# Scores of the latent attention from stacked operands: two products of 128 rows and three of 32 rows for each unit

## The chip, the core and the metric

One core of a Trainium2 chip runs the whole kernel in one launch. The metric is the device time of one execution in microseconds (us). The engines are named as in the profile: PE is TensorE's matmul, PEld its weight load, DVE VectorE, ACT ScalarE, POOL GpSimd, and SP SyncE, whose only work here is to issue DMAs.

## The reference, cut to what matters

The program is a two-layer trunk. Its second layer has a latent attention with 16 heads, 1024 query tokens and 1280 keys (256 of context and 1024 of the sequence). The score of a head has two parts: 64 dimensions of its own ("nope") and 32 rotated dimensions ("rope"), whose keys are shared by all heads.

```
C_HEADS = 16
C_NOPE = 64
C_ROPE = 32
...
def mla_block(q_nope, q_pe, k_nope, k_pe, v):
    scale = (C_NOPE + C_ROPE) ** -0.5
    s = (jnp.einsum('bhqd,bhkd->bhqk', q_nope, k_nope)
         + jnp.einsum('bhqr,bkr->bhqk', q_pe, k_pe)).astype(jnp.float32) * scale
    p = jax.nn.softmax(s, axis=-1)
    return jnp.einsum('bhqk,bhkd->bhqd', p.astype(v.dtype), v)
```

All of it is float32. The kernel splits q and k into a rounded part `hi` and a rest `lo`, and takes hi·hi + hi·lo + lo·hi for a product.

## The kernel before

`project_heads` computes q, k and v and stores them in DRAM, q and k as hi and lo parts: 64 rows for each head's nope dimensions, and behind them the rope rows (32 for each head in q, 32 in all in k). `latent_attention` then goes through 128 units. A unit is one head and 128 query tokens, so a head has 8 units; its scores are 128 x 1280, in three chunks of keys (512, 512 and 256 wide), one PSUM bank each. Two units make a pair, and there are 64 pairs.

A chunk of scores is one `exact_product`: three matmuls (lines 88, 89 and 90) over 96 rows (64 nope and 32 rope rows, stacked). DVE takes the maximum of a unit's scores (line 2956), ACT the exponential (line 2926). PE turns the 10 blocks of 128 x 128 of the result in three groups of 4, 4 and 2 (`turned`, line 2870, with one more block in line 2874 for the inverse sums), ACT and DVE copy them out of PSUM (lines 2934 and 2964), and PE multiplies a pair's blocks with the values (`product`, line 2888). That product goes, for the two units of the pair, to two column halves of 64 each. DVE multiplies it with the inverse sums (`output`, line 2980).

Each engine has its own program, and semaphores join them. PE's order in a pair p is written out by hand; a = 2p and b = 2p + 1 are its units, and scores run two units ahead. A unit's scores need the exponential of the unit two before, since there are two score buffers. Turned groups and products take turns in two PSUM banks: `bank_free` makes PE wait until the fill two before has been read. So group 0 of unit b waits for `output(p - 1)` on DVE, since the product is the fill two before it, and group 1 of unit b waits for ACT's copy of group 2 of unit a.

SP loads a head's q and k with `load_head`: 6 DMAs on one side of a double buffer, issued when the last unit of the head before the one in use has its scores, which is 8 units ahead of their use. The first head's operands are loaded already in `project_heads` (with the shared rope rows, 8 DMAs, `FIRST_LOADS`).

Of the kernel before, what the change touches and what calls it, by code (L numbers as in the profile page):

```python
# [9 lines left out]
F32 = mybir.dt.float32  # L10
# [5 lines left out]
P = 128  # L16
# [20 lines left out]
C_NOPE = 64  # L37
C_ROPE = 32
C_V = 64
C_Q_RANK = 768  # L40
C_KV_RANK = 256
C_IN = C_Q_RANK + C_KV_RANK + C_ROPE
# [41 lines left out]
def exact_product(pe, out, a_hi, a_lo, b_hi, b_lo, first, last):  # L84

    pe.matmul(out, a_hi, b_hi, start=first, stop=False)  # L88
    pe.matmul(out, a_hi, b_lo, start=False, stop=False)  # L89
    return pe.matmul(out, a_lo, b_hi, start=False, stop=last)  # L90
# [2270 lines left out]
                        pool.tensor_tensor(rstd, ms, minus_half[:, :], ALU.pow).then_inc(s.p_rstd.sem, 1)  # L2361


FIRST_LOADS = 8


def load_head(sp, h, q, k, q_parts, k_parts, signal):

    for dst, src in ((k[0], k_parts[0]), (q[0], q_parts[0]), (q[1], q_parts[1]), (k[1], k_parts[1])):
        sp.dma_start(dst[0:C_NOPE, :].bitcast(F32), src[h * C_NOPE:(h + 1) * C_NOPE, :]).then_inc(signal, 16)  # L2370
    first = C_HEADS * C_NOPE + h * C_ROPE
    for dst, src in zip(q, q_parts):
        sp.dma_start(dst[C_NOPE:C_NOPE + C_ROPE, :].bitcast(F32), src[first:first + C_ROPE, :]).then_inc(signal, 16)


def load_positions(sp, k, k_parts, signal):

    for dst, src in zip(k, k_parts):
        sp.dma_start(dst[C_NOPE:C_NOPE + C_ROPE, :].bitcast(F32),
                     src[C_HEADS * C_NOPE:C_HEADS * C_NOPE + C_ROPE, :]).then_inc(signal, 16)  # L2380


def project_heads(nc, q_parts, k_parts, v_rows, cq, ckv, k_pe, w_uq, w_ukv, cos, sin, turn, q_first, k_first, first_in):


    CK, KK = C_Q_RANK // P, C_KV_RANK // P
    HD = C_NOPE + C_ROPE
    SCALE = HD ** -0.5
    k_chunks, q_chunks = token_chunks(T), token_chunks(SEQ)
    GROUP = 4  # L2390
# [348 lines left out]

def latent_attention(nc, y_hi, y_lo, q_parts, k_parts, v_rows, ident, w_raw, w_out, q_first, k_first, first_in):  # L2740

    HD = C_NOPE + C_ROPE
    KT = TT
    UNITS = C_HEADS * XT
    PAIRS = UNITS // 2
# [28 lines left out]
    with ExitStack() as ctx:  # L2774
        def sb(label, shape, dt=F32):
            return ctx.enter_context(nc.sbuf_tensor(f"mla_{label}", shape, dt))

        qs = q_first, [sb(f"q_{n}", [HD, SEQ], F32R) for n in ("hi", "lo")]
        ks = k_first, [sb(f"k_{n}", [HD, T], F32R) for n in ("hi", "lo")]
        v = sb("v", [P, 2, KT, C_V])  # L2780
        e = sb("e", [P, E_SLOTS, T])
        pt = sb("pt", [P, 2, 2, KT, P])
# [6 lines left out]
        s_ps = ctx.enter_context(nc.psum_tensor("mla_scores", [P, 2, 3 * BANK], F32))  # L2789
        t_ps = ctx.enter_context(nc.psum_tensor("mla_turned", [P, 2, BANK], F32))  # L2790
        s = ctx.enter_context(stage(nc, "mla", [
            "pe_in", "qk0_in", "qk1_in", "v0_in", "v1_in", "w_in", "s_full", "max", "exp", "inverted", "inv_spread", "t_full",
            "copied_vector", "copied_scalar", "o_done", "y_rounded", "y_done"], inherited=[first_in]))
        qk_in, v_in = (s.qk0_in, s.qk1_in), (s.v0_in, s.v1_in)
        QK_LOADS = 6
        block = ctx.enter_context(nc.Block())

        @block.sync
        def _(sp):
            def head(h):  # L2800
                if h >= 2:
                    sp.wait_ge(s.s_full.sem, (h - 1) * XT)
                load_head(sp, h, qs[h % 2], ks[h % 2], q_parts, k_parts, qk_in[h % 2].sem)

            def values(h):
                if h >= 2:
                    sp.wait_ge(s.o_done.sem, (h - 1) * PER_HEAD)
                sp.dma_start(v[:, h % 2, :, :],
                             v_rows.rearrange("(t p) n -> p t n", p=P)[:, :, h * C_V:(h + 1) * C_V])\
                  .then_inc(v_in[h % 2].sem, 16)  # L2810

            values(0)
            load_positions(sp, ks[1], k_parts, s.pe_in.sem)
            head(1)
            values(1)
            for h in range(2, C_HEADS):
                head(h)
                values(h)
                if h == 4:
                    for k in range(KD):  # L2820
                        sp.dma_start(w_raw[:, k, :], w_out[k * P:(k + 1) * P, :]).then_inc(s.w_in.sem, 16)
            sp.wait_ge(s.w_in.sem, 16 * KD)

        @block.tensor
        def _(pe):
            def scores(n, c):
                h, t = divmod(n, XT)
                if n >= UNITS:
                    return
                if c == 0:  # L2830
                    if n == 0:
                        pe.wait_ge(first_in, 16 * FIRST_LOADS)
                    elif t == 0:
                        pe.wait_ge(qk_in[h % 2].sem, 16 * QK_LOADS * ((h + 1) // 2))
                        if h == 1:
                            pe.wait_ge(s.pe_in.sem, 32)
                    if n >= 2:
                        pe.wait_ge(s.exp.sem, n - 1)
                a, width = chunks[c]
                tokens = slice(t * P, (t + 1) * P)  # L2840
                (q_hi, q_lo), (k_hi, k_lo) = qs[h % 2], ks[h % 2]
                mm = exact_product(pe, s_ps[:, n % 2, a:a + width], q_hi[:, tokens], q_lo[:, tokens],
                                   k_hi[:, a:a + width], k_lo[:, a:a + width], True, True)
                if c == len(chunks) - 1:
                    mm.then_inc(s.s_full.sem, 1)

            def bank_free(f):

                pair, at = divmod(f - 2, FILLS)
                if f < 2:  # L2850
                    return
                if at == PRODUCT and pair == 0:
                    at = 0
                if at == PRODUCT:
                    pe.wait_ge(s.o_done.sem, pair)
                    return
                unit, group = ((0, 0), (0, 1), None, (0, 2), (1, 0), (1, 1), (1, 2))[at]
                vector, scalar = copies(pair * 2 + unit, group)
                if (unit, group) in by_vector:
                    pe.wait_ge(s.copied_vector.sem, vector)  # L2860
                else:
                    pe.wait_ge(s.copied_scalar.sem, scalar)

            def turned(n, g):
                f = fill(n, g)
                if g == 0:
                    pe.wait_ge(s.exp.sem, n + 1)
                bank_free(f)
                for m, kt in enumerate(groups[g]):
                    mm = pe.transpose(t_ps[:, f % 2, m * P:(m + 1) * P], e[:, n % E_SLOTS, kt * P:(kt + 1) * P],  # L2870
                                      ident[:, :])
                if n % 2 and g == 2:
                    pe.wait_ge(s.inv_spread.sem, n // 2 + 1)
                    mm = pe.transpose(t_ps[:, f % 2, 2 * P:3 * P], inv_rows[:, n // 2 % 2, :], ident[:, :])
                mm.then_inc(s.t_full.sem, 1)

            def product(pair):
                f = product_fill(pair)
                h = pair // PER_HEAD
                bank_free(f)  # L2880
                vector, scalar = copies(2 * pair + 1, 2)
                pe.wait_ge(s.copied_vector.sem, vector)
                pe.wait_ge(s.copied_scalar.sem, scalar)
                if pair % PER_HEAD == 0:
                    pe.wait_ge(v_in[h % 2].sem, 16 * (h // 2 + 1))
                for kt in range(KT):
                    for half in range(2):
                        mm = pe.matmul(t_ps[half * C_V:(half + 1) * C_V, f % 2, 0:P], v[:, h % 2, kt, :],
                                       pt[:, pair % 2, half, kt, :], start=kt == 0, stop=kt == KT - 1)
                mm.then_inc(s.t_full.sem, 1)  # L2890

            for n in range(2):
                for c in range(len(chunks)):
                    scores(n, c)
            for p in range(PAIRS):
                a, b = 2 * p, 2 * p + 1
                scores(a + 2, 0)
                turned(a, 0)
                scores(a + 2, 1)
                turned(a, 1)  # L2900
                scores(a + 2, 2)
                if p:
                    product(p - 1)
                turned(a, 2)
                scores(b + 2, 0)
                turned(b, 0)
                scores(b + 2, 1)
                turned(b, 1)
                scores(b + 2, 2)
                turned(b, 2)  # L2910
            product(PAIRS - 1)
# [119 lines left out]
def trunk(nc, i, consts, ropes, out):  # L3031
# [15 lines left out]
    with ExitStack() as ctx:  # L3047
# [42 lines left out]
        mla_v = scratch("mla_v", T, C_HEADS * C_V)  # L3090
        with ExitStack() as layer1:
            first_head = ExitStack()
            q_first, k_first = ([first_head.enter_context(nc.sbuf_tensor(f"{name}_first_{part}", [C_NOPE + C_ROPE, n],
                                                                     F32R, side="right")) for part in ("hi", "lo")]
                                for name, n in (("q", SEQ), ("k", T)))
            first_in = nc.alloc_semaphore(name="first_in")
            project_heads(nc, q_parts, k_parts, mla_v, cq, ckv, k_pe, i.c_w_uq[0], i.c_w_ukv[0], ropes[2], ropes[3],
                          turn_c, q_first, k_first, first_in)
# [53 lines left out]
```

## Time and profile before

| what | value |
|---|---|
| time of three runs | median 3620.37 us (3615.41 to 3621.24) |
| the profiled execution | 3610.87 us, its span 3609.1 us |
| mean granted TensorE clock | 0.960 of full speed |
| latent attention in the span | from 2200.6 us to about 2741 us, 540 us |
| PE busy over the whole span | 3310.6 us, 92% |

The span goes from the first to the last instruction of one execution. Busy time of PE is taken from modelled ends of pipelined matmuls, so a matmul's duration is longer than its share of a steady stream: the stream is read from the starts of neighbouring instructions.

### The profile page before, as it was taken

Reading aid. Unit: us, or ns where it says so; the run is one execution under the profiler, and the core shown is the slowest. Engines: PE = TensorE matmul, PEld = TensorE weight load, DVE = VectorE, ACT = ScalarE, POOL = GpSimd, SP = SyncE. Lnnn points to the kernel's source line nnn. Section 1 sums busy time; section 2 is a strip of 40 time slices with the busy share of each in tenths; the row PEclk is TensorE's granted clock in tenths of the full one; section 3 lists DMA queues with packets and bytes.
Section 4 is the critical chain, followed back from the end, with each engine's and each line's share of the span. In section 5 each row is a group of like instructions: output and inputs, shape, how many; then the busy total and the mean of one; then the engine's idle time right before and its main releaser. Section 6 shows DMA issues by size and latency. Waiting matters only on the chain. (4 is left out here: it accounts for less than half of the span.)

```text
span 3609.1 us, 47628 instructions
## 1 busy us (share of the span) xinstructions
PE 3310.6 (92%) x18952; PEld 2774.3 (77%) x18952; DVE 1823.9 (51%) x2092; ACT 1166.5 (32%) x1908; POOL 294.7 (8%) x527
## 2 busy tenths in 40 slices
PE   3999599798999999999979698999999799999998
PEld 1787477677888888888869577888887688888886
DVE  4599666454344443444453434555554444444446
ACT  2212155456211111111146323555554322112122
POOL 1000000112000000000012111111111200000001
PEclk6999799889999999999989899999999899999999
DMA  4322587242211111111042743322212311111113
GB/s 183 80 84 98 161 280 245 100 126 87 55 53 35 35 35 35 35 41 41 30 136 84 278 156 94 103 56 49 60 41 77 77 59 52 47 46 58 35 47 117
DMA packets 277081, 316.29 MB, mean 88 GB/s; under 512 B 83824, under 2 KB 222672, under 8 KB 275904
## 3 DMA queue, kind: packets, MB, share of 16 engines
q1 hardware_dynamic: 264160, 267.09, 24.8%
q0 software_dynamic: 12768, 47.08, 3.5%
q8 instruction: 106, 1.74, 0.2%
q14 instruction: 47, 0.39, 0.0%
HBM read 243.54 MB, written 70.58 MB: 87 GB/s over the span
## 5 line engine op out<-in xcount | busy, mean ns | idle before, releaser
L1102 DVE TENSOR_TENSOR y_sum<-ffn_down_ps,y_sum 128x512 f32<-128x512 f32 x396 | 271.1, 690 | 235.7 <-PE ffn_down_ps L90 235.0
L88 PE MATMUL ffn_gate_ps<-y_hi,ffn_w_hi 128*128 128x512 f32 (+1 forms) x880 | 325.5, 370 | 19.0 <-DVE ffn_w_lo L1055 19.0
L88 PE MATMUL ffn_down_ps<-ffn_w_hi,ffn_act_hi 128*128 128x512 f32 x792 | 312.4, 394 | 16.8 <-DVE y_sum L1102 10.4
L89 PE MATMUL ffn_gate_ps<-y_lo,ffn_w_hi 128*128 128x512 f32 (+1 forms) x880 | 325.1, 369 | 0.0
L90 PE MATMUL ffn_gate_ps<-y_hi,ffn_w_lo 128*128 128x512 f32 (+1 forms) x880 | 324.7, 369 | 0.0
L89 PE MATMUL ffn_val_ps<-y_lo,ffn_w_hi 128*128 128x512 f32 (+1 forms) x880 | 323.9, 368 | 0.0
L88 PE MATMUL ffn_val_ps<-y_hi,ffn_w_hi 128*128 128x512 f32 (+1 forms) x880 | 323.8, 368 | 0.0
L90 PE MATMUL ffn_val_ps<-y_hi,ffn_w_lo 128*128 128x512 f32 (+1 forms) x880 | 323.7, 368 | 0.0
L89 PE MATMUL ffn_down_ps<-ffn_w_lo,ffn_act_hi 128*128 128x512 f32 x792 | 309.4, 391 | 0.0
L90 PE MATMUL ffn_down_ps<-ffn_w_hi,ffn_act_lo 128*128 128x512 f32 x792 | 309.1, 390 | 0.0
L1055 DVE TENSOR_TENSOR ffn_w_lo<-ffn_raw,ffn_w_hi 128x1024 fp32r<-128x1024 f32 x132 | 158.0, 1223 | 286.4 <-ACT ffn_w_hi L1014 286.4
L1035 ACT ACTIVATE ffn_act_hi<-ffn_conv 128x1024 fp32r<-128x1024 f32 x66 | 53.4, 840 | 593.3 <-DVE ffn_conv L1082 593.3
L2956 DVE TENSOR_REDUCE mla_neg_max<-mla_scores 128x1 f32<-128x1280 f32 x128 | 190.2, 1486 | 52.6 <-PE mla_scores L90 52.6
L1068 DVE TENSOR_SCALAR ffn_conv<-ffn_gate,ffn_taps 128x1281 f32<-128x1281 f32 (+1 forms) x44 | 38.8, 883 | 341.7 <-ACT ffn_gate L1024 341.7
L2870 PE MATMUL mla_turned<-ident,mla_e 128*128 128x128 f32 x1280 | 206.3, 275 | 1.9 <-ACT mla_pt L2934 1.3
L2926 ACT ACTIVATE mla_e<-mla_scores,mla_neg_max 128x1280 f32<-128x1280 f32 x128 | 170.0, 1328 | 111.6 <-DVE mla_neg_max L2956 111.6
L88 PEld LDWEIGHTS ffn_gate_ps<-y_hi,ffn_w_hi 128*128 128x128 f32 x880 | 166.7, 189 | 48.0 <-DVE ffn_w_lo L1055 19.8
L1014 ACT ACTIVATE ffn_w_hi<-ffn_raw 128x1024 fp32r<-128x1024 f32 x132 | 134.4, 1048 | 209.2 <-PE ffn_val_ps L90 195.6
L88 PEld LDWEIGHTS ffn_down_ps<-ffn_w_hi,ffn_act_hi 128*128 128x128 f32 x792 | 149.1, 188 | 59.1 <-DVE y_sum L1102 21.9
L2870 PEld LDWEIGHTS mla_turned<-ident,mla_e 128*128 128x128 f32 x1280 | 156.2, 141 | 48.1 <-issue 11.8
L666 DVE SCALAR_TENSOR_TENSOR ab_conv<-ab_u,ab_taps,ab_conv 128x1295 f32<-128x1295 f32 x120 | 188.1, 1567 | 3.2
L89 PEld LDWEIGHTS ffn_gate_ps<-y_lo,ffn_w_hi 128*128 128x128 f32 x880 | 166.7, 189 | 28.1
(299 smaller groups left out, 7007.0 us busy)
## 6 DMA issues: line engine op xcount, KB each, us to landing
ffn_raw<-in_ffn_w_up SPq DMA_DIRECT2D x88, 512.0 KB, 3.8
da_ada_w<-in_ada_w SPq DMA_DIRECT2D x10, 4096.0 KB, 24.8
ffn_raw<-in_ffn_w_down SPq DMA_DIRECT2D x44, 512.0 KB, 5.7
ab_raw<-in_ab_w_in SPq DMA_DIRECT2D x20, 512.0 KB, 3.8
mod_ada_w<-in_ada_w SPq DMA_DIRECT2D x4, 2048.0 KB, 11.3
scratch_mla_q_hi<-up_out_hi POOLq DMA_DIRECT2D x12, 512.0 KB, 2.9
scratch_mla_q_lo<-up_out_lo POOLq DMA_DIRECT2D x12, 512.0 KB, 3.2
scratch_qk_hi<-ab_qk_hi POOLq DMA_DIRECT2D x8, 640.0 KB, 3.2
```

Source lines behind the costliest of these rows:

```text
L88: pe.matmul(out, a_hi, b_hi, start=first, stop=False)
L89: pe.matmul(out, a_hi, b_lo, start=False, stop=False)
L90: return pe.matmul(out, a_lo, b_hi, start=False, stop=last)
L666: dve.scalar_tensor_tensor(out=out, in0=src[:, j:j + SPAN], scalar=taps[:, i, j:j + 1], in1=out, op0=ALU.mult, op1=ALU.add)\
L1014: act.activation(w_hi[:, kind, :], raw[:, kind, :], ACT.Copy).then_inc(s.w_hi_done, 1)
L1035: act.activation(act_hi[:, slot, b:b + m], conv[:, padded(b):padded(b) + m], ACT.Copy)\
L1055: dve.tensor_tensor(w_lo[:, kind, :], raw[:, kind, :], w_hi[:, kind, :].bitcast(F32), ALU.subtract).then_inc(s.w_ready, 1)
L1068: dve.tensor_scalar(inner, gate[:, 1:PAD - 1], here, bias, ALU.mult, ALU.add)\
L1102: dve.tensor_tensor(part, down_ps[:, half, :], part, ALU.add).then_inc(s.sum_done, 1)
L2870: mm = pe.transpose(t_ps[:, f % 2, m * P:(m + 1) * P], e[:, n % E_SLOTS, kt * P:(kt + 1) * P], ident[:, :])
L2926: act.activation(e[:, n % E_SLOTS, :], s_ps[:, n % 2, 0:T], ACT.Exp, bias=neg_max[:, n:n + 1], accum_out=sums[:, n:n + 1]).then_inc(s.exp. ...
L2956: dve.tensor_reduce(neg_max[:, n:n + 1], s_ps[:, n % 2, 0:T], AX.X, ALU.max, negate=True)\
```

## The change

The rows of hi·hi, hi·lo and lo·hi (3 x 96 for each chunk) are stacked anew, as 128, 128 and 32. The left operand of product 0 is q's nope hi (64 rows), q's rope hi (32) and the first 32 rows of q's nope lo; of product 1 it is q's nope hi, q's rope hi and the second 32 rows of q's nope lo. The right operands are k's nope hi, k's rope hi and the first 32 rows of k's nope hi; and k's nope lo, k's rope lo and the second 32 rows of k's nope hi. What is left is q's rope lo with k's rope hi, 32 rows. For each chunk that is one matmul more, and the three chunks take it from three separate groups of 32 rows (0 to 31, 32 to 63, 64 to 95), for which q's rope lo is loaded three times and k's rope hi is laid out once as `k_rope`.

```
-                mm = exact_product(pe, s_ps[:, n % 2, a:a + width], q_hi[:, tokens], q_lo[:, tokens],
-                                   k_hi[:, a:a + width], k_lo[:, a:a + width], True, True)
+                q, k = qs[h % 2], ks[h % 2]
+                for m in range(2):
+                    pe.matmul(s_ps[:, n % 2, a:a + width], q[m][:, tokens], k[m][:, a:a + width], start=m == 0,
+                              stop=False)
                 if c == len(chunks) - 1:
+
+                    for m, (a, width) in enumerate(chunks):
+                        rows = slice(m * BLOCK, (m + 1) * BLOCK)
+                        mm = pe.matmul(s_ps[:, n % 2, a:a + width], q[2][rows, tokens], k_rope[rows, 0:width],
+                                       start=False, stop=True)
                     mm.then_inc(s.s_full.sem, 1)
```

A head's loads become 13 DMAs (for the first head 15 with the shared rows), and three loads of `k_rope` stand first in SP's program of the stage; unit 0's scores wait for them:

```
+HEAD_LOADS = 13
+POSITION_LOADS = 2
+FIRST_LOADS = HEAD_LOADS + POSITION_LOADS
...
+    for n in range(2):
+        some = slice(h * C_NOPE + n * BLOCK, h * C_NOPE + (n + 1) * BLOCK)
+        load(k[n], 0, k_parts[n], nope)
+        load(q[n], 0, q_parts[0], nope)
+        load(q[n], C_NOPE, q_parts[0], rope)
+        load(q[n], HD, q_parts[1], some)
+        load(k[n], HD, k_parts[0], some)
+    for n in range(3):
+        load(q[2], n * BLOCK, q_parts[1], rope)
...
+            for c, (a, width) in enumerate(chunks):
+                sp.dma_start(k_rope[c * BLOCK:(c + 1) * BLOCK, 0:width].bitcast(F32),
+                             k_parts[0][C_HEADS * C_NOPE:C_HEADS * C_NOPE + C_ROPE, a:a + width])\
+                  .then_inc(s.rope_in.sem, 16)
...
                     if n == 0:
                         pe.wait_ge(first_in, 16 * FIRST_LOADS)
+                        pe.wait_ge(s.rope_in.sem, 16 * len(chunks))
```

And the order of PE's work in a pair is another. Six blocks of scores become three:

```
             for p in range(PAIRS):
                 a, b = 2 * p, 2 * p + 1
-                scores(a + 2, 0)
                 turned(a, 0)
-                scores(a + 2, 1)
+                for c in range(len(chunks)):
+                    scores(a + 2, c)
                 turned(a, 1)
-                scores(a + 2, 2)
                 if p:
                     product(p - 1)
                 turned(a, 2)
                 scores(b + 2, 0)
                 turned(b, 0)
+                turned(b, 1)
                 scores(b + 2, 1)
-                turned(b, 1)
                 scores(b + 2, 2)
                 turned(b, 2)
```

On PE, from the last chunk of unit a's scores to group 0 of unit b, the program before reads:

```order
L88 MATMUL mla_scores<-k_first_hi,q_first_hi 128x256
L89 MATMUL mla_scores<-k_first_lo,q_first_hi 128x256
L90 MATMUL mla_scores<-k_first_hi,q_first_lo 128x256
L2888 MATMUL mla_turned<-mla_pt,mla_v 64x128 x20
L2870 MATMUL mla_turned<-ident,mla_e 128x128 x2
L88 MATMUL mla_scores<-k_first_hi,q_first_hi 128x512
L89 MATMUL mla_scores<-k_first_lo,q_first_hi 128x512
L90 MATMUL mla_scores<-k_first_hi,q_first_lo 128x512
L2870 MATMUL mla_turned<-ident,mla_e 128x128 x4
```

And the changed one, from unit a's scores to the end of unit b's (line 2861 is now the product over 128 rows, line 2867 the one over 32 rows, 2894 `turned`, 2912 `product`):

```order
L2861 MATMUL mla_scores<-k_first,q_first 128x512 x4
L2861 MATMUL mla_scores<-k_first,q_first 128x256 x2
L2867 MATMUL mla_scores<-mla_k_rope,q_first 128x512 x2
L2867 MATMUL mla_scores<-mla_k_rope,q_first 128x256
L2894 MATMUL mla_turned<-ident,mla_e 128x128 x4
L2912 MATMUL mla_turned<-mla_pt,mla_v 64x128 x20
L2894 MATMUL mla_turned<-ident,mla_e 128x128 x2
L2861 MATMUL mla_scores<-k_first,q_first 128x512 x2
L2894 MATMUL mla_turned<-ident,mla_e 128x128 x8
L2861 MATMUL mla_scores<-k_first,q_first 128x512 x2
L2861 MATMUL mla_scores<-k_first,q_first 128x256 x2
L2867 MATMUL mla_scores<-mla_k_rope,q_first 128x512 x2
```

Between the product of the values and group 0 of unit b stood three matmuls of 512 columns, and now stand two; each unit has a block of 32-row products between its scores and the next turned group.

On SP, at the start of the stage, the program before reads (the values of head 0, the shared rows, then head 1):

```order
L2808 DMA mla_v<-scratch_mla_v 128x10x64
L2379 DMA mla_k_hi<-scratch_mla_k_hi 32x1280
L2379 DMA mla_k_lo<-scratch_mla_k_lo 32x1280
L2370 DMA mla_k_hi<-scratch_mla_k_hi 64x1280
L2370 DMA mla_q_hi<-scratch_mla_q_hi 64x1024
```

and the changed one:

```order
L2826 DMA mla_k_rope<-scratch_mla_k_hi 32x512 x2
L2826 DMA mla_k_rope<-scratch_mla_k_hi 32x256
L2821 DMA mla_v<-scratch_mla_v 128x10x64
L2394 DMA mla_k_first<-scratch_mla_k_hi 32x1280
L2394 DMA mla_k_second<-scratch_mla_k_lo 32x1280
L2378 DMA mla_k_first<-scratch_mla_k_hi 64x1280
L2378 DMA mla_q_first<-scratch_mla_q_hi 64x1024
```

The three loads of `k_rope` moved in ahead of everything else.

## Rows read from the trace of the kernel before

**Rows 1.** Windows: busy us of each engine (count), PE clock, DMA share, GB/s
```profile
2200.00:2741.00 541.00, 534.57 (x5056) 466.99 (x5056) 314.91 (x448) 305.35 (x577) 90.06 (x192) 1.00 0.26 59
2300.00:2400.00 100.00, 100.00 (x953) 87.56 (x954) 59.06 (x85) 57.37 (x109) 17.01 (x36) 1.00 0.37 98
```

**Rows 2.** Timeline (start us, us, engine ...): one pair, from product to next product
```profile
2349.86 0.28 PE L90 MATMUL mla_scores<-k_first_hi,q_first_lo 96*128 96x256 f32 x1
...
2350.07 2.40 PE L2888 MATMUL mla_turned<-mla_pt,mla_v 128*64 128x128 f32 x40
...
2352.40 0.44 PE L2870 MATMUL mla_turned<-ident,mla_e 128*128 128x128 f32 x2
...
2352.92 0.40 PE L89 MATMUL mla_scores<-k_first_lo,q_first_hi 96*128 96x512 f32 x1
...
2353.39 0.60 PE L2870 MATMUL mla_turned<-ident,mla_e 128*128 128x128 f32 x4
...
2355.08 0.28 PE L89 MATMUL mla_scores<-k_first_lo,q_first_hi 96*128 96x256 f32 x1
...
2355.20 0.28 PE L90 MATMUL mla_scores<-k_first_hi,q_first_lo 96*128 96x256 f32 x1
...
2355.32 0.38 PE L2870 MATMUL mla_turned<-ident,mla_e 128*128 128x128 f32 x2
...
2358.35 2.40 PE L2888 MATMUL mla_turned<-mla_pt,mla_v 128*64 128x128 f32 x40
```

**Rows 3.** One tile: durations min/median/max ns of the product with the values
```profile
L2888 PE MATMUL mla_turned<-mla_pt,mla_v x2560: 272/273/324, 2217.3 to 2739.4; 128*64 128x128 f32 x197
```

**Rows 4.** Timeline in the projection: matmuls on 128 rows, then on 32
```profile
2011.60 0.28 PE L89 MATMUL up_main<-up_ckv_lo,up_wkv_hi 128*128 128x256 f32 x1
2011.72 0.28 PE L90 MATMUL up_main<-up_ckv_hi,up_wkv_lo 128*128 128x256 f32 x1
2011.93 1.90 PE L2543 MATMUL up_main<-up_k_pe,turn_c 32*32 32x512 f32 x4
```

**Rows 5.** One line: durations min/median/max ns of those on 32 rows
```profile
L2543 PE MATMUL up_main<-up_k_pe,turn_c x4: 588/588/612, 2011.9 to 2013.2; 32*32 32x512 f32 x4
```

**Rows 6.** Timeline: scores after a wait, so that the weight load is bare
```profile
2207.18 0.50 PE L88 MATMUL mla_scores<-k_first_hi,q_first_hi 96*128 96x512 f32 x1 [1.11 <-ACT mla_e L2926]
...
2207.52 0.40 PE L89 MATMUL mla_scores<-k_first_lo,q_first_hi 96*128 96x512 f32 x1
```

**Rows 7.** Timeline in the last pair: product, output, group 0 of unit b
```profile
2731.52 2.40 PE L2888 MATMUL mla_turned<-mla_pt,mla_v 128*64 128x128 f32 x40 [0.79 <-DVE mla_pt L2964]
...
2733.97 0.59 DVE L2980 TENSOR_TENSOR mla_o<-mla_turned,mla_inv_t 64x128 f32<-64x128 f32 x2 [1.46 <-PE mla_turned L2888]
...
2734.71 1.06 PE L2870 MATMUL mla_turned<-ident,mla_e 128*128 128x128 f32 x8 [0.42 <-DVE mla_o L2980]
```

**Rows 8.** The page, costliest groups: busy us, mean ns of one | idle before
```profile
L2956 DVE TENSOR_REDUCE mla_neg_max<-mla_scores 128x1 f32<-128x1280 f32 x128 | 190.2, 1486 | 52.6 <-PE mla_scores L90 52.6
...
L2926 ACT ACTIVATE mla_e<-mla_scores,mla_neg_max 128x1280 f32<-128x1280 f32 x128 | 170.0, 1328 | 111.6 <-DVE mla_neg_max L2956 111.6
```

**Rows 9.** Timeline at the stage's start, and loads: KB each, us to landing
```profile
2200.57 0.38 SPq L2808 DMA_DIRECT2D mla_v<-scratch_mla_v  x1
2200.61 0.76 PE L88 MATMUL mla_scores<-k_first_hi,q_first_hi 96*128 96x512 f32 x1 [11.06 <-PEq L76]
...
ident<-in_squares SPq DMA_DIRECT2D x1, 64.0 KB, 1.9
...
mla_k_hi<-scratch_mla_k_hi SPq DMA_DIRECT2D x1, 160.0 KB, 4.1
```

**Rows 10.** Timeline of SP: a head's six loads (first, last), the next heads' first
```profile
2231.01 0.45 SPq L2370 DMA_DIRECT2D k_first_hi<-scratch_mla_k_hi  x1
...
2234.33 0.42 SPq L2373 DMA_DIRECT2D q_first_lo<-scratch_mla_q_lo  x1
...
2264.24 0.45 SPq L2370 DMA_DIRECT2D mla_k_hi<-scratch_mla_k_hi  x1
```

More of the change, by code:

```diff
@@ L39 @@
 C_V = 64
+HD = C_NOPE + C_ROPE
 C_Q_RANK = 768
@@ L2361, in _, with load @@
                         pool.tensor_tensor(rstd, ms, minus_half[:, :], ALU.pow).then_inc(s.p_rstd.sem, 1)
-FIRST_LOADS = 8
+HEAD_LOADS = 13
+POSITION_LOADS = 2
+FIRST_LOADS = HEAD_LOADS + POSITION_LOADS
 def load_head(sp, h, q, k, q_parts, k_parts, signal):
[L2369 to L2373, printed above, removed]
+    nope = slice(h * C_NOPE, (h + 1) * C_NOPE)
+    rope = slice(C_HEADS * C_NOPE + h * C_ROPE, C_HEADS * C_NOPE + (h + 1) * C_ROPE)
+    def load(dst, at, src, rows):
+        sp.dma_start(dst[at:at + rows.stop - rows.start, :].bitcast(F32), src[rows, :]).then_inc(signal, 16)
+    for n in range(2):
[7 more added lines that the diff above has]
+        load(q[2], n * BLOCK, q_parts[1], rope)
 def load_positions(sp, k, k_parts, signal):
     for dst, src in zip(k, k_parts):
-        sp.dma_start(dst[C_NOPE:C_NOPE + C_ROPE, :].bitcast(F32),
+        sp.dma_start(dst[C_NOPE:HD, :].bitcast(F32),
                      src[C_HEADS * C_NOPE:C_HEADS * C_NOPE + C_ROPE, :]).then_inc(signal, 16)
@@ L2386, in project_heads @@
     CK, KK = C_Q_RANK // P, C_KV_RANK // P
-    HD = C_NOPE + C_ROPE
     SCALE = HD ** -0.5
@@ L2740, in latent_attention @@
 def latent_attention(nc, y_hi, y_lo, q_parts, k_parts, v_rows, ident, w_raw, w_out, q_first, k_first, first_in):
-    HD = C_NOPE + C_ROPE
     KT = TT
@@ L2776, in sb @@
             return ctx.enter_context(nc.sbuf_tensor(f"mla_{label}", shape, dt))
-        qs = q_first, [sb(f"q_{n}", [HD, SEQ], F32R) for n in ("hi", "lo")]
-        ks = k_first, [sb(f"k_{n}", [HD, T], F32R) for n in ("hi", "lo")]
+        qs = q_first, [sb(f"q_{n}", [P, SEQ], F32R) for n in ("first", "second", "rope")]
+        ks = k_first, [sb(f"k_{n}", [P, T], F32R) for n in ("first", "second")]
+        k_rope = sb("k_rope", [HD, BANK], F32R)
         v = sb("v", [P, 2, KT, C_V])
@@ L2791, in latent_attention @@
         s = ctx.enter_context(stage(nc, "mla", [
-            "pe_in", "qk0_in", "qk1_in", "v0_in", "v1_in", "w_in", "s_full", "max", "exp", "inverted", "inv_spread", "t_full",
+            "pe_in", "rope_in", "qk0_in", "qk1_in", "v0_in", "v1_in", "w_in", "s_full", "max", "exp", "inverted", "inv_spread", "t_full",
             "copied_vector", "copied_scalar", "o_done", "y_rounded", "y_done"], inherited=[first_in]))
         qk_in, v_in = (s.qk0_in, s.qk1_in), (s.v0_in, s.v1_in)
-        QK_LOADS = 6
         block = ctx.enter_context(nc.Block())
@@ L2832, in scores @@
                         pe.wait_ge(first_in, 16 * FIRST_LOADS)
+                        pe.wait_ge(s.rope_in.sem, 16 * len(chunks))
                     elif t == 0:
-                        pe.wait_ge(qk_in[h % 2].sem, 16 * QK_LOADS * ((h + 1) // 2))
+                        pe.wait_ge(qk_in[h % 2].sem, 16 * HEAD_LOADS * ((h + 1) // 2))
                         if h == 1:
-                            pe.wait_ge(s.pe_in.sem, 32)
+                            pe.wait_ge(s.pe_in.sem, 16 * POSITION_LOADS)
                     if n >= 2:
@@ L2840, in scores @@
                 tokens = slice(t * P, (t + 1) * P)
-                (q_hi, q_lo), (k_hi, k_lo) = qs[h % 2], ks[h % 2]
-                mm = exact_product(pe, s_ps[:, n % 2, a:a + width], q_hi[:, tokens], q_lo[:, tokens],
-                                   k_hi[:, a:a + width], k_lo[:, a:a + width], True, True)
+                q, k = qs[h % 2], ks[h % 2]
+                for m in range(2):
+                    pe.matmul(s_ps[:, n % 2, a:a + width], q[m][:, tokens], k[m][:, a:a + width], start=m == 0,
+                              stop=False)
                 if c == len(chunks) - 1:
+                    for m, (a, width) in enumerate(chunks):
+                        rows = slice(m * BLOCK, (m + 1) * BLOCK)
+                        mm = pe.matmul(s_ps[:, n % 2, a:a + width], q[2][rows, tokens], k_rope[rows, 0:width],
+                                       start=False, stop=True)
                     mm.then_inc(s.s_full.sem, 1)
@@ L2896, in _ @@
                 a, b = 2 * p, 2 * p + 1
-                scores(a + 2, 0)
                 turned(a, 0)
-                scores(a + 2, 1)
+                for c in range(len(chunks)):
+                    scores(a + 2, c)
                 turned(a, 1)
-                scores(a + 2, 2)
                 if p:
@@ L2906, in _ @@
                 turned(b, 0)
+                turned(b, 1)
                 scores(b + 2, 1)
-                turned(b, 1)
                 scores(b + 2, 2)
@@ L3092, in trunk @@
             first_head = ExitStack()
-            q_first, k_first = ([first_head.enter_context(nc.sbuf_tensor(f"{name}_first_{part}", [C_NOPE + C_ROPE, n],
-                                                                     F32R, side="right")) for part in ("hi", "lo")]
-                                for name, n in (("q", SEQ), ("k", T)))
+            q_first, k_first = ([first_head.enter_context(nc.sbuf_tensor(f"{name}_first_{part}", [P, n], F32R,
+                                                                     side="right")) for part in range(parts)]
+                                for name, n, parts in (("q", SEQ, 3), ("k", T, 2)))
             first_in = nc.alloc_semaphore(name="first_in")
```

## The prediction

> **What bounds the kernel now.** First the windows [rows 1]: from 2200 to 2741 us PE is busy for 534.57 of 541 us, in the middle of the stage for all of it, at a granted clock of 1.00 (2.4 GHz). DVE and ACT are busy for 315 and 305 us, a good half. So the stage is PE's stream of instructions, and a gain or a loss on PE goes straight into the time, unless it opens a wait. Then the timeline of one pair, read by starts [rows 2]. From one product to the next it is 2358.35 - 2350.07 = 8.28 us. In it a score matmul of 512 columns takes (2353.39 - 2352.92) / 2 = 0.235 us and one of 256 columns (2355.32 - 2355.08) / 2 = 0.12. Four turned blocks start 0.11 apart ((0.60 - 0.27) / 3), and product to next turned group is 2.33. With 12 x 0.235 + 6 x 0.12 = 3.54 of scores, 19 turned blocks at 0.11 (2.09), the product (2.33), the two blocks behind it (0.27) and 0.09 ahead of it (below) the pair is accounted for to 0.04 us: there are no waits to win.
>
> **Two things in that stream price the change.** One is that parts of the array work side by side: 40 instructions of the product start within 2.40 - 0.27 = 2.13 us, one in 0.055 us, although each streams 128 columns of float32, for which a turned block takes 0.11. They are two column halves. The other is what it costs to go there and back. From the last score matmul to the first of the product it is 2350.07 - 2349.86 = 0.21 instead of 0.12, so 0.09 more; the first matmul there lasts 324 instead of 273 ns [rows 3], 0.05 more. On the way back the last product matmul starts at 2350.07 + 2.13 = 2352.20 and the turned block at 2352.40, 0.20 instead of 0.11, and the two turned blocks last 0.44 instead of 0.38: 0.09 + 0.06 [rows 2].
>
> Is that so for 32 rows too? The trace has one place, a matmul of 32 rows and 32 columns behind matmuls of 128 rows: 2011.93 - 2011.72 = 0.21 against 0.12 [rows 4], the same 0.09, and its first lasts 24 ns longer than the others (612 against 588, [rows 5]). That is 24 ns for 32 columns of weights and 51 for 64; with 128 columns it should be 0.10, and a score matmul that finds its weights unloaded does last 0.50 instead of 0.40 [rows 6]. So I take 0.09 on entry, 0.10 for the weights and 0.15 on the way out: 0.34 us each time. The row changes rows and columns at once; that rows alone pay the same I infer.
>
> The Trainium skill says, in "TensorEngine Tiling (Array Packing)", Key Properties, that changing the tiling mode, and not just the tile, drains TensorE. The trace agrees where it has such a change, with 0.09 us at the entry. By the rule each unit pays 0.34 us; without it the block of 32 rows would cost its stream alone, as in rival B.
>
> **The change on PE.** For each of the 128 units it removes one of three matmuls for each chunk: 2 x 0.235 + 0.12 = 0.59 us. It adds three matmuls of 32 rows. If they run side by side they take one stream of 512 columns, 0.235, and 0.01 for the later starts. With 0.34 for the change there and back that is 0.585. Net 0.005 a unit, 0.6 us in all: nothing. The products over 128 rows instead of 96 I take at the same time. The fewer changes between scores and turned blocks gain nothing either, since those show no gap in the account above.
>
> Bounds: without any cost of the change the block is 0.245 (gain 0.345 a unit, 44 us); side by side but with three weight loads in turn it is 0.10 longer (third load 0.20 late but only 0.12 of stream, second 0.10 late and 0.235), 13 us in all; with the products in turn it is 0.235 + 0.12 longer, 45 us.
>
> **The new order.** Group 0 of unit b needs `output` of the pair before. In the last pair, where PE has nothing else to do, it starts 2734.71 - 2731.52 = 3.19 us after the product did, released by that DVE work [rows 7]. Before the change it started at 2353.39, 3.32 after the product: 0.13 to spare. Now two, not three, matmuls of 512 columns stand in between, so PE is there at 3.32 - 0.235 = 3.085 and waits 0.105. In 62 pairs that is 6.5 us, whatever the 32 rows cost. Nothing gives it back, since PE is the bound and the turned groups behind it queue up. The other waits keep their cover: ACT's copy of unit a's group 2, for which group 1 of unit b waits, stands behind an exponential. From the end of unit a + 2's scores it is 1.49 of maximum and 1.33 of exponential [rows 8], and the copy, with the gaps between engines some 3.8 us; PE has 0.44 + 2.33 + 0.27 + 0.47 + 0.44 and the wait in between, 4.05. DVE's copy of group 0, queued behind a maximum, needs 1.49 and the copy from the end of unit b's scores; PE has 0.33 + 0.44 + 1.77 + 0.44 = 3.0 until the product wants that bank.
>
> **SP and the loads.** At the start PE began at 2200.61, when SP only issued its first load [rows 9]. Now unit 0 waits for `k_rope`: third issue 2 x 0.43 later, and a load of 64 KB lands 1.9 us after its issue, 2.8 in all. A load of 160 KB in the stage took 4.1, which would make 5. I take 3.0. Nothing else is on the chip then to hide it. The values of head 0 stand behind them, but their product comes at 2217.3 [rows 3]. A head's loads grow from 6 to 13: the six take 2234.75 - 2231.01 = 3.7 us to issue [rows 10], so 13 take 8, and a load lands some 4 later [rows 9]. The next head's scores start 33.2 us after the issue (2264.24 - 2231.01), so some 20 us are to spare. Bytes grow by about 1.7 for these loads, against a DMA share of 0.26 [rows 1]. The first head's loads, 15 for 8, are issued in the projection as soon as its rows are stored, while PE goes through the other heads' products. All that is hidden, at 0.
>
> **Sum.** 0 + 6.5 + 3.0 = 9.5 us. The profiled execution of 3610.87 us becomes 3620.4, and the median of the runs, 3620.37, which lies 9.5 above that execution, becomes 3629.9. A measurement of this kernel tells some 0.2%, 7 us, from no change, so this would be just slower.
>
> **The rivals.**
>
> B, the rows change nothing: PE takes the block of 32 rows without the cost seen at the column halves, since only rows differ. For it speaks that scores over 96 rows and turned blocks over 128 alternate without any gap [rows 2]; against it the 0.21 of [rows 4]. 9.5 - 44 = -35 us, 3586. The side changes where the block costs less than 0.515 a unit. By the Trainium skill ("TensorE: Matmul & The Clock Gate", Part 3, The mechanism) a weight load for other row groups is pulled ahead of matmuls in flight, which is this case; no row of this trace shows it for rows alone.
>
> B', half of it: one of the two changes is covered or the weights of 32 rows load during the entry. The block costs 0.10 to 0.17 less, 13 to 22 us: 3608 to 3617, faster or the same.
>
> C, the weights of the three load in turn: the block is 0.10 longer, 9.5 + 13 = +22, 3643. Against it speaks that the column halves' first two matmuls cost 0.05 together, the load of one.
>
> D, the three products don't overlap, as the change says they would: 0.355 longer a unit, +45 + 9.5, 3675. What the product shows is overlap of columns; rows into three separate banks are untried in this trace.
>
> Same, the wait at group 0 is not there, because the output's release comes 0.1 sooner than in the last pair, or the entry is a little cheaper: 3623.
>
> **How the numbers follow.** The likeliest, full cost and side by side, has 0.42, and its own range is 3625 to 3638 (block of 0.56 to 0.62, `k_rope` up to 5 us, the wait up to 0.13). B has 0.20, B' 0.14, the last case 0.08, C 0.10, D 0.06. Faster by over 0.2% are B and half of B': 0.27. Slower are C, D and 0.38 of the likeliest: 0.54. The rest, 0.19, is within 0.2%. Leaving out D and the ends of the others, the range is 3585 to 3644.
>
> **What the profile after would show.** Right: two matmuls over 128 rows 0.235 apart, then 0.21 to the first of 32 rows, the three of them starting together and the first lasting 0.10 longer than an ordinary one; the turned block 0.32 or so after their start plus load; PE waiting 0.1 us for `mla_o` before group 0 of unit b; PE's first matmul some 3 us after SP's first load; a pair of 8.4 us. Wrong: a block of 0.25 (pair of 7.7, B), starts of the three 0.235 apart (D) or 0.10 apart (C), or a wait for qk loads at a head's first unit.

## The result and the profile after

| | before | changed |
|---|---|---|
| median of 7 runs | 3620.37 us (3615.41 to 3622.56) | 3630.56 us (3627.06 to 3634.32) |
| ratio | | 1.0031, 95% interval 1.0021 to 1.0040 |
| profiled execution, its span | 3610.87, 3609.1 | 3632.77, 3631.0 |
| a pair: mean distance of neighbouring products' starts, pairs 3 to 58 | 8.302 us | 8.417 us |
| first to last product of the stage | 520.03 us | 526.76 us |
| SP's first load of the stage to PE's first matmul | 0.04 us | 2.79 us |

The change costs 10.2 us, 0.3%. The latent attention accounts for it: 526.76 - 520.03 = 6.7 us between its products and 2.75 at its start are 9.5 us. The two profiled executions lie 21.9 us apart, but 12.4 of these are outside the stage: 8.7 before it and 3.7 behind it. It began at 2209.29 instead of 2200.57, and before that the two programs do the same work but for the first head's seven more loads. In the other kernels with this projection the stage began between 2202.1 and 2213.5. In all of them the difference arose in the projection's first 80 us or earlier, before those loads are issued. So the loads are not its cause, and the medians, 10.2 us apart, leave at most a small part of it to the change. From the last product to the end of the span all ten kernels do the same work, and take between 871 and 876 us. Whether there is such a part the two profiled executions with the old projection (before and e5_order_alone, with stage starts at 2200.57 and 2205.68, and both at the lower end behind the stage) don't settle.

The timeline of the changed kernel, one pair from the end of unit a's scores on (start us, us, engine, line; compare [rows 2]):

```profile
2732.36 0.28 PE L2861 MATMUL mla_scores<-mla_k_first,mla_q_first 128*128 128x256 f32 x1
2732.48 0.28 PE L2861 MATMUL mla_scores<-mla_k_second,mla_q_second 128*128 128x256 f32 x1
2732.69 0.50 PE L2867 MATMUL mla_scores<-mla_k_rope,mla_q_rope 32*128 32x512 f32 x3
2733.12 0.66 PE L2894 MATMUL mla_turned<-ident,mla_e 128*128 128x128 f32 x4
...
2733.70 2.40 PE L2912 MATMUL mla_turned<-mla_pt,mla_v 128*64 128x128 f32 x40
...
2736.04 0.44 PE L2894 MATMUL mla_turned<-ident,mla_e 128*128 128x128 f32 x2
2736.15 0.59 DVE L3003 TENSOR_TENSOR mla_o<-mla_turned,mla_inv_t 64x128 f32<-64x128 f32 x2 [1.23 <-PE mla_turned L2912]
...
2736.55 0.40 PE L2861 MATMUL mla_scores<-mla_k_second,mla_q_second 128*128 128x512 f32 x1
...
2736.89 0.52 PE L2894 MATMUL mla_turned<-ident,mla_e 128*128 128x128 f32 x3
```

The entry is there: 2732.69 - 2732.48 = 0.21 us to the first product of 32 rows instead of 0.12. All three of them fit in 0.50 us, the duration of one, so they run side by side. The next turned group starts 0.43 after them, and its four blocks last 0.66 instead of 0.60, the bare weight load. Block and both changes are 0.09 + 0.43 + 0.06 = 0.58 us. Then, 2736.89 - 2733.70 = 3.19 after the product, group 0 of unit b starts. (The row counts only the blocks that begin before the window ends; the two groups have eight.) Its place in PE's queue was free at 2736.55 + 0.235 = 2736.79, so it waited 0.10 us for `mla_o`: it starts 0.15 after the second `output` ends (2736.15 + 0.59), as in [rows 7]. No wait is named in brackets on that row: PE's busy time, with its modelled ends, hides a gap this small, and only starts show it.

By tile, the durations of one product of 32 rows (min/median/max ns):

```profile
L2867 PE MATMUL mla_scores<-mla_k_rope,mla_q_rope x192: 377/490/500, 2244.5 to 2747.0; 32*128 32x512 f32 x128, 32*128 32x256 f32 x64
```

490 ns is 0.10 more than a 512-column score matmul's 0.39 to 0.40: each of them has its weight load bare (not hidden behind an earlier matmul), but at the same time.

At the stage's start PE waits for the three loads, and a head's 13 loads later take 2250.30 - 2242.58 = 7.7 us to issue, from 4 pairs or 34 us ahead of their use on:

```profile
2209.29 1.23 SPq L2826 DMA_DIRECT2D mla_k_rope<-scratch_mla_k_hi  x3
...
2212.08 2.47 PE L2861 MATMUL mla_scores<-k_first,q_first 128*128 128x512 f32 x6 [13.80 <-DMA mla_k_rope<-scratch_mla_k_hi]
...
2242.58 0.45 SPq L2378 DMA_DIRECT2D k_first<-scratch_mla_k_hi  x1
...
2248.95 1.35 SPq L2378 DMA_DIRECT2D q_first<-scratch_mla_q_lo  x3
```

A window of 100 us in mid stage (busy us of PE, PEld, DVE, ACT, POOL, each with its count, then clock, DMA share, GB/s) shows PE as full as before at the same granted clock (compare [rows 1]), and more DMA:

```profile
2300.00:2400.00 100.00, 100.00 (x943) 79.62 (x941) 60.10 (x84) 59.28 (x108) 16.25 (x35) 1.00 0.49 126
```

### The profile page after: what moved, and what is told of

Read it like the earlier page. It is cut to its first block and busy times, and to the rows that moved or that the text cites. A ratio compares the mean times of both kernels' runs of the same rounds, so it can differ in the third digit from the quotient of the medians.

```text
span 3631.0 us, 47744 instructions
## 1 busy us (share of the span) xinstructions
PE 3327.8 (92%) x18952; PEld 2744.6 (76%) x18952; DVE 1830.1 (50%) x2092; ACT 1179.3 (32%) x1908; POOL 294.1 (8%) x527
## 5 line engine op out<-in xcount | busy, mean ns | idle before, releaser
L91 PEld LDWEIGHTS ffn_gate_ps<-y_hi,ffn_w_lo 128*128 128x128 f32 x880 | 167.1, 190 | 28.1
```

## The experiments

The theory: going to 32 rows and back costs as much as the products saved, the stage's 9.5 us are a wait of PE for the output of the pair before (in every pair) and the loads of `k_rope` (once). Rivals: the blocks of 32 rows or the order itself cost the time; the three products do not overlap. What is read of each kernel, all in us:

| kernel | a pair | first and last product | between them | median of its runs |
|---|---|---|---|---|
| before | 8.302 | 2217.27, 2737.30 | 520.03 | 3620.37 |
| changed | 8.417 | 2228.72, 2755.48 | 526.76 | 3630.56 |
| e1_late | 8.269 | 2227.36, 2745.00 | 517.64 | 3619.32 |
| e2_one_group | 9.102 | 2229.28, 2798.17 | 568.89 | 3674.99 (one) |
| e3_left_out | 7.288 | 2227.07, 2684.51 | 457.44 | 3558.66 (one) |
| e4_wait_at_use | 8.415 | 2231.11, 2757.73 | 526.62 | 3635.18 (one) |
| e5_order_alone | 8.268 | 2222.58, 2740.30 | 517.72 | 3613.14 (one) |
| e6_products_alone | 8.267 | 2227.56, 2745.16 | 517.60 | 3619.86 (one) |
| e7_block_at_product | 8.271 | 2224.66, 2742.55 | 517.89 | 3619.85 (one) |
| e8_adjacent | 8.127 | 2225.96, 2734.91 | 508.95 | 3604.25 |

Single times vary by as much as 14 us for one kernel, so where there is one, the pair decides.

**e1_late: take the wait away.** Work already there is moved into the gap.

```
                 scores(b + 2, 0)
+                scores(b + 2, 1)
                 turned(b, 0)
                 turned(b, 1)
-                scores(b + 2, 1)
```

> The changed kernel with the second chunk of unit b's scores moved ahead of its turned groups 0 and 1 (one more 0.47 us of scores between the product and group 0). Theory (PE waits 0.1 us in each pair for the output of the pair before): group 0 no longer waits, and a pair goes from 8.417 to about 8.30 us, 7 us less in all, 3623. Rival (the 0.115 us a pair come from the blocks of 32 rows, and the wait only stands where PE would have lost the time anyway): a pair stays at 8.42 and the time at 3630.

```profile
2367.94 2.40 PE L2912 MATMUL mla_turned<-mla_pt,mla_v 128*64 128x128 f32 x40
2370.27 0.44 PE L2894 MATMUL mla_turned<-ident,mla_e 128*128 128x128 f32 x2
2370.47 1.18 PE L2861 MATMUL mla_scores<-k_first,q_first 128*128 128x512 f32 x4
2371.49 1.03 PE L2894 MATMUL mla_turned<-ident,mla_e 128*128 128x128 f32 x8
```

In its timeline group 0 starts 3.55 us after the product, past the 3.19 at which the output is ready. A pair takes 8.269: 0.148 less than in the changed kernel, more than the 0.115 expected, and even 0.03 less than before. The median is 3619.32 against 3620.18 of the kernel before in the same comparison, ratio 0.9993 (0.9984 to 1.0002): with this one move the change costs nothing that can be measured.

**e2_one_group: take the overlap away.** All three products of 32 rows use rows 0 to 31.

```
-                        mm = pe.matmul(s_ps[:, n % 2, a:a + width], q[2][rows, tokens], k_rope[rows, 0:width],
+                        mm = pe.matmul(s_ps[:, n % 2, a:a + width], q[2][0:BLOCK, tokens], k_rope[:, a:a + width],
```

> The changed kernel with all three products of 32 rows taken from the same rows 0 to 31, so that they cannot run side by side. Theory (side by side in separate rows, so that three cost one stream): each block grows by 0.235 + 0.12 us, a pair from 8.42 to 9.13, some 45 us in all, 3675. Rival (the three starts 3 ns apart in the trace only show their issue, and PE streams them one after another in either form): a pair stays at 8.42.

```profile
2407.10 0.84 PE L2866 MATMUL mla_scores<-mla_k_rope,mla_q_rope 32*128 32x512 f32 x3
2407.87 0.44 PE L2893 MATMUL mla_turned<-ident,mla_e 128*128 128x128 f32 x2
```

From the block to the next turned group it is 0.77 us instead of 0.43, and a pair takes 0.685 more, 0.34 a block. The products overlap in separate rows and not in the same ones.

**e3_left_out: the price of the block.** The products of 32 rows are left out of the scores.

```
-                    for m, (a, width) in enumerate(chunks):
-                        rows = slice(m * BLOCK, (m + 1) * BLOCK)
-                        mm = pe.matmul(s_ps[:, n % 2, a:a + width], q[2][rows, tokens], k_rope[rows, 0:width],
-                                       start=False, stop=True)
```

> The changed kernel without the products of 32 rows (q's rope rest times k's rope is left out of the scores); their operands are still loaded. Theory (a block costs its stream of 0.235 us and 0.33 for going to 32 rows and back, 0.57 in all): a pair goes from 8.42 to about 7.28 us, 72 us less in all. If only the stream counted, it would go to 7.95, 30 us less. DVE and ACT, busy for a good half, should not yet bind; if they do, the pair stays above 7.28 with waits of PE for them.

```profile
2401.45 0.60 PE L2889 MATMUL mla_turned<-ident,mla_e 128*128 128x128 f32 x4
...
2406.27 0.69 DVE L2982 COPY mla_pt<-mla_turned 128x512 f32<-128x512 f32 x1 [1.25 <-PE mla_turned L2889]
...
2407.11 0.63 PE L2889 MATMUL mla_turned<-ident,mla_e 128*128 128x128 f32 x4
```

A pair takes 7.288 us: 1.129 less, or 0.565 a block by plain halving. But with the blocks gone this kernel has a small wait that the changed one has not. Group 0 of unit a starts 0.15 us after DVE's copy of unit b's group 1 ends (2406.27 + 0.69 to 2407.11), the distance of group 0 of unit b from `output` in [rows 7], and its four blocks last 0.63 instead of 0.60. Over pairs 3 to 58 the wait and the slower first block come to 0.03 us a pair. So a block costs (1.129 + 0.03) / 2 = 0.58 us, as the starts of the changed kernel gave above; in the half of the pair where no such wait falls, the same instructions take 0.584 less by their starts. Of the 0.58, 0.235 is stream and the rest, some 0.345, is the way to 32 rows and back.

**e4_wait_at_use: the stage's start.** Unit 0 waits for `k_rope` only ahead of its first product of 32 rows.

```
-                        pe.wait_ge(s.rope_in.sem, 16 * len(chunks))
...
+                    if n == 0:
+                        pe.wait_ge(s.rope_in.sem, 16 * len(chunks))
```

> The changed kernel with the wait for k_rope moved from unit 0's first product to its first product of 32 rows. Theory (the stage starts 2.8 us late for these loads): PE starts with SP again, its six products over 128 rows take 2.4 us at half clock while the loads land, and the first product of the values comes some 19.4 us after the stage's start becomes 16.9, 2.4 us sooner. Rival (head 0's units are held by something else that is late at the start, such as ACT's table or the values): the first product of the values stays 19.4 us after SP's first load.

```profile
2213.52 1.23 SPq L2826 DMA_DIRECT2D mla_k_rope<-scratch_mla_k_hi  x3
...
2213.56 2.47 PE L2860 MATMUL mla_scores<-k_first,q_first 128*128 128x512 f32 x6 [11.07 <-PEq L77]
...
2216.09 0.79 PE L2868 MATMUL mla_scores<-mla_k_rope,q_first 32*128 32x512 f32 x3
2216.81 2.50 PE L2860 MATMUL mla_scores<-k_first,q_first 128*128 128x512 f32 x6
```

PE starts with the stage. From SP's first load (2213.52) to the first product it is 17.6 us, 1.8 less than the 19.4 of the changed kernel and not 2.4: the rival, by which it stays at 19.4, fell, and the gain is smaller than expected. The windows of 2 us show why, in the column after POOL's: the granted clock is still at its low level (0.50, 1.2 GHz) until eight us after PE's first matmul,

```profile
2217.50:2219.50 2.00, 2.00 (x9) 1.49 (x7) 0.93 (x1) 1.04 (x1) 0.00 (x0) 0.50 1.06 235
2219.50:2221.50 2.00, 2.00 (x9) 1.47 (x10) 1.41 (x2) 0.38 (x2) 0.00 (x0) 0.50 1.03 217
2221.50:2223.50 2.00, 2.00 (x13) 1.31 (x11) 1.14 (x3) 1.42 (x2) 0.00 (x0) 0.96 1.03 230
```

where in the changed kernel, whose PE began at 2212.08, it rose between four and six us after (0.69 is the mean of a window in which it rose):

```profile
2216.00:2218.00 2.00, 1.98 (x8) 1.25 (x7) 0.82 (x1) 1.15 (x1) 0.00 (x0) 0.69 1.03 222
2218.00:2220.00 2.00, 1.68 (x10) 1.44 (x10) 1.97 (x2) 0.72 (x3) 0.00 (x0) 1.00 1.08 238
```

So some of what starting early gains is spent at the low clock. These are single executions, and the clock differs from one to the next. e8 (below) starts as e4 does and also takes 17.6 us; e1 and e6 start as the changed kernel and take 18.9 and 19.3, but e7 and e2, which start so too, take 22.6 and 25.5. In e7 the clock fell back to the low level 11.8 us after PE's first matmul and stayed there for 6.8 (first two rows), in e2 it rose only after 18.8 us (third row):

```profile
2209.90:2216.60 6.70, 4.81 (x31) 3.33 (x29) 3.65 (x4) 4.29 (x7) 0.29 (x1) 1.00 1.05 226
2216.80:2223.40 6.60, 6.29 (x22) 4.96 (x23) 2.88 (x3) 2.71 (x6) 0.00 (x0) 0.50 0.53 97
2215.00:2225.20 10.20, 9.51 (x31) 7.25 (x31) 3.55 (x5) 4.20 (x7) 0.29 (x1) 0.50 0.67 135
```

The distances from the first to the last product, in the table above, begin after these stretches.

**e8_adjacent: one return less.** Group 1 of unit a goes ahead of its third chunk, so that the block of 32 rows stands at the product; with e1's and e4's edits.

```
+                scores(a + 2, 0)
+                scores(a + 2, 1)
-                for c in range(len(chunks)):
-                    scores(a + 2, c)
                 turned(a, 1)
+                scores(a + 2, 2)
                 if p:
                     product(p - 1)
                 turned(a, 2)
                 scores(b + 2, 0)
+                scores(b + 2, 1)
                 turned(b, 0)
                 turned(b, 1)
-                scores(b + 2, 1)
```

> The changed kernel in an order in which unit a's block of 32 rows stands directly ahead of the product with the values (turned group 1 moved ahead of the third chunk), group 0 of unit b stands behind the second chunk of its scores, and unit 0 waits for k_rope only at its first product of 32 rows. Theory (each return to 128 rows costs 0.09 us and 0.055 of bare weight load, and going from 32 rows to the column halves costs one entry only): a pair goes from the 8.269 of the late form to about 8.12 us, below the 8.302 of before; 63 x 0.18 = 11 us less than before, 1 us more at the start, so 3610. Rival (32 rows to column halves costs both an exit and an entry): a pair stays at 8.27 and the time at 3618.

```profile
2396.19 0.50 PE L2868 MATMUL mla_scores<-mla_k_rope,mla_q_rope 32*128 32x512 f32 x3
2396.61 2.40 PE L2913 MATMUL mla_turned<-mla_pt,mla_v 128*64 128x128 f32 x40
...
2398.95 0.44 PE L2895 MATMUL mla_turned<-ident,mla_e 128*128 128x128 f32 x2
...
2400.16 1.04 PE L2895 MATMUL mla_turned<-ident,mla_e 128*128 128x128 f32 x8
```

The product starts 0.42 us after the block, as a turned group would: from 32 rows to column halves is one change, not two. A pair takes 8.127 us, 0.142 less than in e1. The median is 3604.25 against 3618.45 of before, ratio 0.9957 (0.9944 to 0.9971): this version beats the kernel before, by 14.2 us where 10 were expected. The stage accounts for 10.2 of them (508.95 against 520.03, and 0.9 more up to the first product); the other 4 are outside it and not explained.

**e5_order_alone: the old products in the new order** (the hunk of the order in the diff above, applied to the kernel before).

> The kernel before with its three products of 96 rows, in the order of the changed one. Theory (three blocks of scores instead of six gain nothing, and three matmuls of 512 columns cover the output that group 0 of unit b waits for, by 0.13 us): a pair stays at 8.30 us. Rival (the order itself costs the 0.115 us): 8.42. Rival (fewer changes between scores and turned blocks gain): under 8.27.

```profile
2371.46 2.40 PE L2888 MATMUL mla_turned<-mla_pt,mla_v 128*64 128x128 f32 x40
...
2374.78 1.04 PE L2870 MATMUL mla_turned<-ident,mla_e 128*128 128x128 f32 x8
```

Group 0 starts 3.32 us after the product, so nothing waits. A pair takes 8.268, 0.034 less than before and just under the 8.27 of the second rival: the order costs nothing, and my figure of no gain was wrong. With the products of 96 rows, three blocks of scores instead of six save 0.034 us, 0.011 for each block that falls away.

**e6_products_alone: the new products in the old order** (that hunk taken back).

> The changed products in the order of the kernel before, six blocks of scores. Theory (the wait comes from the two matmuls that are left between the product and group 0, which this order has too): group 0 starts 3.19 us after the product and a pair takes 8.42 us as in the changed kernel. Rival (the wait comes from the new order): a pair takes 8.27 to 8.30.

```profile
2400.69 0.49 PE L2867 MATMUL mla_scores<-mla_k_rope,mla_q_rope 32*128 32x512 f32 x3
2401.11 2.40 PE L2912 MATMUL mla_turned<-mla_pt,mla_v 128*64 128x128 f32 x40
...
2404.30 0.63 PE L2894 MATMUL mla_turned<-ident,mla_e 128*128 128x128 f32 x4
```

The wait is there as expected (2404.30 - 2401.11 = 3.19), but the pair takes 8.267 and not 8.42. The expectation missed what its rows show: in the old order the third chunk, and so the block of 32 rows, stands directly ahead of the product. A new theory, that this saves one return, and the next run tests it alone. It leaves 0.035 us open: a saved return and a wait that cancel would give the 8.30 of the kernel before, not 8.267.

**e7_block_at_product: that alone, in the changed kernel.**

```
-                for c in range(len(chunks)):
-                    scores(a + 2, c)
+                scores(a + 2, 0)
+                scores(a + 2, 1)
                 turned(a, 1)
+                scores(a + 2, 2)
```

> The changed kernel with one move: turned group 1 of unit a stands ahead of the third chunk of unit a's scores, so that the block of 32 rows is followed directly by the product with the values. The wait of group 0 is left as it is. Theory (the old order with the new products took 8.267 us a pair, in spite of the wait, because its block of 32 rows stands at the product and one return to 128 rows falls away, 0.09 + 0.055): a pair goes from 8.417 to about 8.27 us, and group 0 still starts 3.19 us after the product. Rival (the old order won it elsewhere, by spreading the scores in six blocks): a pair stays at 8.42.

```profile
2406.20 0.49 PE L2867 MATMUL mla_scores<-mla_k_rope,q_first 32*128 32x512 f32 x3
2406.62 2.40 PE L2912 MATMUL mla_turned<-mla_pt,mla_v 128*64 128x128 f32 x40
```

A pair takes 8.271 us, 0.146 less, with the wait still in place (group 0 again 3.19 after the product). It has four blocks of scores and e6 has six, with the same products and the same wait, and e6 is no slower (8.267): the 0.011 a block of e5 is not seen with the new products. Three such blocks, from the changed kernel's three to e6's six, are the 0.035 that e6 left open. Why they cost nothing here no run shows. The four kernels close: 8.417 with both costs, 8.269 and 8.271 with one of them, 8.127 with neither.

## Why the prediction was right

It forecast 3629.9 us and slower; 3630.56 was measured. By its steps:

- **PE bounds the stage.** Right: PE is busy in the whole of the mid-stage window after the change too, and each edit of its stream came out in the pair within 0.05 us of its price, but for e6 with its new neighbour of the block.
- **The products against the block.** I set 0.59 removed against 0.585 added, net nothing. e1 and e5 have the same order but for one chunk, no wait at group 0 and the block away from the product, and differ by 8.269 - 8.268 = 0.001 us a pair: the products and the block do cancel. For the block the starts and e3, with its small wait counted, give 0.58 where I had 0.585.
- **The cost of going to 32 rows.** I inferred it from one matmul of 32 rows and 32 columns, and from the column halves. Right for rows alone: 0.21 on entry, 0.10 of bare weights, some 0.345 in all (0.34 forecast). This agrees with what the Trainium skill says in "TensorEngine Tiling (Array Packing)", Key Properties, that a changed mode drains TensorE; the price is these runs' alone. Rival B, by which the weights would be pulled ahead, fell, and its half B' with it. The sentence of the Trainium skill behind it did not fit the entry in the first place: it is of loads for row groups other than those in use, and the matmul ahead, of 128 rows, uses all of them. Among the three themselves the weights do load together, so rival C fell too, and D fell with e2.
- **The wait at group 0.** Right in place and mechanism, to 0.01 us in the start after the product (3.19). Its price was too small: I had 0.105, and e1 shows 0.148. A turned group that waited also starts with bare weights, as the scores in [rows 6] do; its first start-to-start distance is 0.03 longer. The last 0.015 I can't place.
- **The order.** I gave the fewer alternations nothing. With the products of 96 rows they gain 0.034 us a pair (e5), 2 us in all. By luck this offset most of what the wait was under-priced by: 0.148 - 0.034 = 0.114 a pair where I had 0.105. Between the stage's first and last product that is 6.7 us, where I had 6.5.
- **A step I did not see:** the new order takes the block of 32 rows away from the product, where the old one would have had it. That costs 0.146 us a pair (e7), 9 us in all, as much as the whole loss. It didn't harm the sum, since the kernel before has no such block; it is why the change of products alone (e6) doesn't show the wait in its pair.
- **Start and loads.** 2.8 us measured at PE's first matmul and 2.7 at the first product, 3.0 forecast. With the clock as it varies there from one execution to the next, the latter is one sample. A head's 13 loads take 7.7 us to issue, 8 forecast, and no head's first unit waited for them.

So 9.2 (wait) - 2.1 (order) + 0 (products) + 2.8 (start) = 9.9, with 9.5 in the stage by the two traces and 10.2 in the medians. The way is from the kernel before over e5 and e1 to the changed one; in another order of the steps the 0.035 of e6 falls elsewhere.

## What to carry to other kernels

A stream of instructions on a full PE can be priced from starts of neighbours in the trace, here to 0.01 us for a block and 0.04 for a pair, also for a form that is not yet there, if each way in and out is counted: packing small products into separate row groups won 0.34 us a block here and paid as much for the way there and back. Group the packed work so that one way serves more of it, next to other packed work (here the product in column halves) rather than among products of the full array. And when a stream gets shorter, look for the results that it used to cover by a margin smaller than the cut: 0.13 us were to spare, and 0.235 were taken.

## What the runs showed of the hardware that I had not expected

- From products of 32 rows straight to products in column halves costs one change: 0.42 us from the block's start to the product's in e8, e6 and e7, against 0.43 to a turned group. The return to the full array in between, with its second entry, is what falls away, 0.142 to 0.146 us.
- Three weight loads of 128 columns for three row groups lie bare at the same time: all three products last 0.49 to 0.50, and together 0.50.
- Going between turned blocks and scores of 96 rows has a small price after all, 0.011 us for each block of scores (e5). With the new products it is not seen (e6 against e7).
- When the clock rises after the idle start of the stage is not fixed: about 4 us after PE's first matmul in the kernel before, 5 in the changed one, 8 in e4 and e8, each with PE busy all the while but for about 0.1 us, and 19 in e2, with PE idle for 0.7. It can also fall back: in e7 after 6.8 us at the full clock, of which PE was idle for 1.9 (window under e4).
